# First block: both pairs of norms of the even layer and of its MLP taken in two waves of tokens

## What is computed

```python
def rms_norm(x, g): return x * lax.rsqrt(jnp.mean(x * x, -1, keepdims=True) + EPS) * g
# layer i = 0; the same for the context with its own shifts, scales and gates
h = modulate(rms_norm(x, norm_g[0, 0]), sh1, sc1)
y = even_mixer(h, hc, ...)                         # ends in a product with ev_w_out
x = x + gt1 * rms_norm(y, norm_g[0, 1])            # norm pair A: norm of y ...
h = modulate(rms_norm(x, norm_g[0, 2]), sh2, sc2)  # ... then norm of the new x
x = x + gt2 * rms_norm(squared_relu_mlp(h, mlp_w1[0], mlp_w2[0]), norm_g[0, 3])   # norm pair B
# layer i = 1
h = modulate(rms_norm(x, norm_g[1, 0]), sh1, sc1)
# odd_mixer: near = mean of the two neighbouring tokens of h, xx = near - h,
# and its keys are (h + xx * mu[2]) @ rw_wk, with five more such mixes after it
```

## Time and profile before

| | |
|---|---|
| median of 3 runs | 4765.43 us (4764.15 to 4767.18) |
| the profiled execution | 4766.37 us |
| its span, first to last instruction | 4764.6 us |
| PE busy | 4546.2 us, 95% of the span |
| DVE busy | 2705.9 us, 57% |
| ACT busy | 1044.7 us, 22% |
| POOL busy | 81.2 us, 2% |
| mean granted PE clock | 0.971 of full |
| share of PE in the chain that ended last | 87% |

### The profile page before, as it was taken

How to read it: one execution, slowest core, us unless ns; L and a number is a source line. 1 busy time by engine, 2 the same in 40 slices (tenths; PEclk the granted TensorE clock), 3 DMA queues, 4 the chain that set the end, 5 groups by cost and what they waited for, 6 DMA issues and landing times.

```text
span 4764.6 us, 70102 instructions
## 1 busy us (share of the span) xinstructions
PE 4546.2 (95%) x29830; PEld 3211.4 (67%) x29830; DVE 2705.9 (57%) x4827; ACT 1044.7 (22%) x2337; POOL 81.2 (2%) x81
## 2 busy tenths in 40 slices
PE   7999999998999999999999999989999999989998
PEld 4556555555546676756886888545887888545886
DVE  3163445535336777744565666674657666674656
ACT  1052000002016666631002100251001000151000
POOL 0000000000000000000000000110000000020000
PEclk9998999998999999998999999989999999989999
DMA  5301222210200000111222212211222212211221
GB/s 240 124 28 53 89 102 101 112 75 36 84 1 3 3 3 3 38 46 71 89 89 74 89 71 80 106 36 71 89 89 80 89 71 80 102 40 71 89 89 45
DMA packets 27045, 339.08 MB, mean 71 GB/s; under 512 B 3024, under 2 KB 3024, under 8 KB 6896
## 3 DMA queue, kind: packets, MB, share of 16 engines
q1 hardware_dynamic: 24048, 324.51, 18.1%
q0 software_dynamic: 2688, 10.09, 0.6%
HBM read 330.40 MB, written 4.19 MB: 70 GB/s over the span
## 4 chain that ended last, share of the span: by engine, by line
PE 87%; DVE 7%; ACT 3%; issue 2%; DMA 1%; SPq 0%; ACTq 0%; DVEq 0%
PE ps L1402 46%; PE ps L1086 22%; PE ps L1095 2%; PE ps L1602 1%; PE ps L1182 1%; PE ps L1533 1%; PE ps L1574 1%; PE ps L1585 1%; PE ps L1139 1%; ACT arena L1856 1%; PE ps L1340 1%; PE ps L1662 1%; PE ps L1471 1%; DVE arena L2951 1%; DMA arena<-in_panels 1%
## 5 line engine op out<-in xcount | busy, mean ns | idle before, releaser
L1402 PE MATMUL ps<-arena 128*128 128x256 f32 (+1 forms) x9096 | 2118.3, 395 | 20.8 <-DVE arena L2707 20.8
L1402 PEld LDWEIGHTS ps<-arena 128*128 128x128 f32 x9096 | 1735.4, 191 | 391.4 <-DVE arena L2707 23.6
L1086 PE MATMUL ps<-arena 128*128 128x512 f32 (+3 forms) x2896 | 1066.6, 529 | 2.2 <-ACT arena L1807 1.8
L1086 PEld LDWEIGHTS ps<-arena 128*128 128x128 f32 x2896 | 542.0, 191 | 514.7 <-issue 366.1
L2698 DVE TENSOR_TENSOR arena<-ps,arena 128x512 f32<-128x512 f32 (+1 forms) x250 | 157.6, 630 | 318.7 <-PE ps L1402 317.0
L2698 DVE TENSOR_TENSOR square<-ps,square 128x512 f32<-128x512 f32 (+1 forms) x145 | 99.1, 684 | 177.3 <-PE ps L1402 177.2
L2639 DVE TENSOR_TENSOR arena<-arena 128x1024 f32<-128x1024 f32 (+2 forms) x153 | 190.5, 1245 | 8.7 <-ACT arena L1807 5.4
L1997 ACT COPY square<-ps 128x512 f32<-128x512 f32 (+1 forms) x65 | 37.2, 573 | 658.0 <-PE ps L1402 589.1
L1997 ACT COPY arena<-ps 128x384 f32<-128x384 f32 (+1 forms) x35 | 18.5, 529 | 575.1 <-PE ps L1402 549.2
L2959 DVE COPY_PREDICATED arena<-const,ps 128x256 f32<-128x256 int32 x192 | 83.8, 445 | 74.9 <-PE ps L1602 69.4
L1856 ACT ACTIVATE arena<-arena,state_sum 128x256 f32<-128x256 f32 (+2 forms) x128 | 76.5, 598 | 213.7 <-DVE state_sum L2426 211.7
(11 more groups left out here) (348 smaller groups left out, 4924.5 us busy)
## 6 DMA issues: line engine op xcount, KB each, us to landing
arena<-in_panels SPq DMA_DIRECT2D x144, 2048.0 KB, 7.7
arena<-in_panels SPq DMA_DIRECT2D x9, 1536.0 KB, 6.4
arena<-in_bias POOLq DMA_DIRECT2D x8, 512.0 KB, 4.5
arena<-in_x_in SPq DMA_DIRECT2D x1, 3072.0 KB, 11.1
x_save<-arena POOLq DMA_DIRECT2D x1, 2048.0 KB, 7.5
arena<-x_save POOLq DMA_DIRECT2D x1, 2048.0 KB, 13.0
out_x<-arena SPq DMA_DIRECT2D x8, 256.0 KB, 2.2
arena<-in_panels SPq DMA_DIRECT2D x1, 1792.0 KB, 11.7
```

Source lines behind the costliest of these rows:

```text
L1086: ins = pe.matmul(dest, left(k), right(k), start=(k == 0), stop=(k == nk - 1))
L1402: ins = pe.matmul(bank[:, j * cut.side:(j + 1) * cut.side], left[:, k, j * P:(j + 1) * P], right[k], start=(k == 0), stop=(k == cut.rows - 1))
```

## The change

It replaces project, post and norm_mod at turn A by one step, out_turn, and the last down group, post and norm_mod(1, 0) at turn B by the same code inside mlp and odd_in. The tokens are split as WAVES: latents (512), then context (256). In PE's order, from the diff:

- Both panels of the closing product are held at once (load_pair; SLOT is changed for the panels of turn A so that they lie in slots 1 and 2 and the first up panel in slot 0; their slots are given free only when all 16 tiles are done). All eight chunks of latents come first, then the eight of context. After the first chunk of context PE makes the latents' first sum (wave_sum "post"), after the second their row, after the seventh the second sum ("norm"), after the eighth the second row. DVE and ACT do the latents' additions, squares and gates between the emptying of the context's tiles.
- Squares for the second norm are gathered too: POOL adds chunks 1 to 6 (norm_gather), so the second sum takes 16 records for the latents and 8 for the context instead of 96 together.
- The context's two sums and two rows lie inside the next product over the latents: at turn A inside the first up panel (first_up: four chunks together, sums and rows after k = 0, 2, 4, 6, then the context of the panel), at turn B inside the keys (after k = 1, after the first panel, and inside the second panel).
- POOL saves X after the latents' addition; the waits on x_chunk elsewhere are recounted.

```diff
-                SLOT.append(p % RING)
+                SLOT.append(p % RING if p < MLP_PANEL[0] - 2 else p - MLP_PANEL[0] + 3)
+        WAVES = ((0, LAT), (LAT, TOK))
-            e["project"](2, SEG2, Y, Z, "attn")
-            e["post"](Z, 0, 1)
-            e["norm_mod"](0, 2)
+            e["out_turn"]()
...
+            def turn(src):                                    # PE
+                latents, context = WAVES[0:1], WAVES[1:2]
+                w0 = panel()
+                columns(w0, range(4), src, latents)
+                w1 = panel()
+                columns(w1, range(4), src, latents)
+                columns(w0, [0], src, context)
+                wave_sum("post", 0)
+                columns(w0, [1], src, context)
+                wave_row(0)
+                columns(w0, [2, 3], src, context)
+                columns(w1, [0, 1, 2], src, context)
+                wave_sum("norm", 0)
+                columns(w1, [3], src, context)
+                wave_row(0)
...
+            def first_up(w):                                  # PE, turn A
+                banks = [tile() for _ in range(4)]
+                for k in range(KD):
+                    pe.wait_ge(sem("h_act"), more("h_act"))
+                    for m, bank in enumerate(banks):
+                        ins = pe.matmul(bank, w[:, k, m * P:(m + 1) * P], H[:, k, 0:LAT], start=(k == 0), stop=(k == KD - 1))
...
+                    if k == 0:
+                        wave_sum("post", 1)
+                    elif k == 2:
+                        wave_row(1)
+                    elif k == 4:
+                        wave_sum("norm", 1)
+                    elif k == 6:
+                        wave_row(1)
+                together(w, range(4), H, WAVES[1:2], "h_act")
...
                 for k in range(KD):                           # PE, odd_in
                     pe.wait_ge(sem("mix"), more("mix"))
...
+                    if k == 1:
+                        wave_sum("post", 1)
+                wave_row(1)
+                w1 = panel()
+                columns(w1, [0, 1], MIX, WAVES[0:1])
+                wave_sum("norm", 1)
+                columns(w1, [2], MIX, WAVES[0:1])
+                wave_row(1)
+                columns(w1, [3], MIX, WAVES[0:1])
+                together(w0, range(4), MIX, WAVES[1:2], "mix")
+                columns(w1, range(4), MIX, WAVES[1:2])
...
+            def norm_gather(v):                               # POOL
+                for c in range(1, KD - 1):
+                    pool.wait_ge(sem("squared"), base + c + 1)
...
+                    pool.tensor_tensor(rstd[:, a:b], rstd[:, a:b], square[:, c % 2, a:b], ALU.add).then_inc(
...
+            def turn(src, evacuate):                          # DVE
+                for c in range(KD):
+                    evacuate(c, *WAVES[0])
+                    wave_gather(c - 1, 0)
+                evacuate(0, *WAVES[1])
+                wave_root(0)
+                evacuate(1, *WAVES[1])
+                dve.wait_ge(sem("row"), more("row"))
+                for c in range(KD):
+                    wave_times(src, c, 0)
+                    if c > 0:
+                        wave_add(src, c - 1, 0, n["own"] - 1)
+                    if c % 2 == 1:
+                        evacuate(2 + c // 2, *WAVES[1])
+                        wave_gather(1 + c // 2, 1)
+                wave_add(src, KD - 1, 0, n["own"])
+                evacuate(6, *WAVES[1])
+                wave_gather(5, 1)
+                wave_root(0)
+                evacuate(7, *WAVES[1])
+                wave_gather(6, 1)
+                dve.wait_ge(sem("row"), more("row"))
```

More of the change, by code:

```diff
@@ L1199, in gathered_sum, with wave_sum @@
                 ins.then_inc(sem("summed"), one("summed"))
+            def wave_sum(kind, v):
+                a, b = WAVES[v]
+                squares, gathered = dict(post=("square", "gathered"), norm=("squared", "norm_gathered"))[kind]
+                stat_bank_free()
+                pe.wait_ge(sem(squares), more(squares, KD))
+                pe.wait_ge(sem(gathered), more(gathered, KD - 2))
+                for t in range(a // P, b // P):
+                    for c in (0, KD - 1):
+                        ins = pe.matmul(ps[:, 4, 0:TILES], square_dest(c)[:, t * P:(t + 1) * P], to_column(t),
+                                        start=(t == a // P and c == 0), stop=(t == b // P - 1 and c == KD - 1))
+                ins.then_inc(sem("summed"), one("summed"))
@@ new lines, in wave_row @@
+            def wave_row(v):
+                a, b = WAVES[v]
+                pe.wait_ge(sem("spread"), more("spread"))
+                for t in range(a // P, b // P):
+                    ins = pe.transpose(token_row(TOK)[:, t * P:(t + 1) * P], rstd[:, t * P:(t + 1) * P], ident)
+                ins.then_inc(sem("row"), one("row"))
+            def turn(src):
[13 more added lines that the diff above has]
+                wave_row(0)
@@ L1355, in mlp @@
                     kind, g, part = item
+                    if beside and (kind, g) == LAST_DOWN:
+                        if part == 0:
+                            pe.wait_ge(sem("half_hidden"), ends[g][0])
+                            pe.wait_ge(sem("tile_free"), ends[g][1])
+                            turn(hidden1[g % 2])
+                        continue
                     w = panel()
@@ L1370, in mlp @@
                         between = None
[L1371 to L1375, removed]
+                    if beside and item == ("up", 0, 0):
+                        first_up(w)
+                    elif not fast:
+                        columns(w, range(4), src, segs, KD, None if kind == "down" else "h_act")
                     if kind == "up":
@@ L1906, in mlp @@
                         continue
+                    if beside and (kind, g) == LAST_DOWN:
+                        if part == 0:
+                            turn(Y, 3, 1, 0)
+                        continue
                     fast = cuts(item, FF1_GROUPS, beside)
@@ new lines, in out_turn, with evacuate @@
+            def out_turn():
+                def evacuate(c, a, b):
+                    dve.tensor_copy(Z[:, c, a:b], tile()[:, 0:b - a]).then_inc(sem("tile_free"), one("tile_free"))
+                turn(Z, evacuate)
+                for c in range(KD):
+                    wave_scale(c, 0)
+                wave_root(1)
+                dve.wait_ge(sem("row"), more("row"))
+                wave_result(Z, 1)
+                wave_root(1)
+                dve.wait_ge(sem("row"), more("row"))
+                for c in range(KD):
+                    wave_scale(c, 1)
+                n["h_act"] += 2 * KD
+                n["square"] += 2 * KD
+                n["gated"] += 2 * KD
+                n["squared"] += 2 * KD
```

265 lines of the change are left out of this document (219 added, 46 removed).

## The result

The kernel after took **4726.23 us** (median of 5, 4720.35 to 4728.06) beside 4766.43 (4764.15 to 4768.05, 5 runs) of the kernel before: a ratio of 0.9913, 95% interval 0.9903 to 0.9923. It is faster by 40.2 us, where the prediction's two gains came to 50.1. The profiled execution took 4725.82 us.

A forecast was written before the change was run, and what follows sets the result against it. PE bounds the kernel, idle at turns A and B for 39.0 and 41.2 us plus clock losses. Gains of 23.9 and 26.2 us off the median 4765.4 gave 4715.3 us; forecast band 4710 to 4721, wide range 4705 to 4730.

The forecast's parts named there:

- Splitting the products costs nothing: Both turns: records of 512 and 256 columns take 0.645 us together against 0.647 for two of 384; eight chunks stay 82.6.
- Sums and rows: Each turn: two sums and two rows for latents and for context, 8.2 us of PE, all on the path.
- The latents' second sum: Both turns: POOL's clashes cost DVE 0 to 4.9 us, mostly absorbed by waits for tiles; 0.2 us of stall taken.
- The context's sum in first_up: Turn A, middle of the first up panel: 1.2 us of stall from DVE's gathers, clashes with POOL and a square.
- Handover behind the second row at A: Turn A: PE waits 1.6 us for the first chunk of H: one scale, two left-over gates and one modulation.
- The four banks: Turn A, end of first_up's latents: PE waits 4.2 us for four banks, behind ACT's modulations, relus and a DVE product.
- The clock: Each turn: 2.5 us lost to the low clock behind the long wait, nothing charged for short waits.
- Edits costed at nothing: Both turns: moved panel loads and POOL's save of the latents are covered by other work and cost nothing.
- Rival 1: POOL's additions become the last term of a sum, price 6 to 10 us: 4721 to 4726; chance 0.13.
- Rival 2: Handover waits are smaller and the clock doesn't fall: 4705 to 4710; chance 0.13.
- Rival 3: Handovers are longer through a missed wait in ACT's or DVE's order, 5 to 10 us a turn: 4726 to 4738; chance 0.10.
- Rival 4: Low clock lasts behind the turns' rows, products at 1.2 GHz, up to 124 us lost: 4839; chance 0.04.

The follow-up runs named there:

- Experiment 1: Kernel after with each of POOL's additions for the second norms cut to 64 columns, so those sums are partial: 4717.5 us, run once.
- experiment 4: Kernel after with DVE's gatherings of the context's first-norm squares moved behind the latents' last addition, ACT's squares and gates moved to match: 4720.67 us, run once.
- experiment 8: Kernel after with late gatherings, latents' relus between the context's modulations, and a key tile emptied one mix earlier, together: 4710.31 us, ratio 0.9880.
- experiment 7: The kernel after, unchanged, measured again on another chip: 4723.54 us, ratio 0.9909 to the kernel before.

## Why the prediction came out as it did

The direction was right, and so was where the gain lies; 4715.3 was 11 us too low. The time lies in the wide range, 4705 to 4730, and outside the forecast's own band of 4710 to 4721, which had been given 0.58: two terms were too small in each turn. By the steps of the forecast:

- **Splitting the products costs nothing**: right. The eight chunks of latents and the first of context take 58.65 us, 8 x 6.87 + 3.45 = 58.4.
- **Sums and rows**, 8.2 us a turn: too high. The records read 1.68 + 0.44 for the latents' first, 1.92 + 0.44, 0.79 + 0.23 and 1.03 + 0.23: 6.8 us, and 6.5 in turn B, where neither sum of the context stands behind a wait. The row of 0.77 in the earlier trace rows is four transposes with a little waiting in it; set among products they take 0.44.
- **The latents' second sum**, 0.2 us of stall: wrong, 1.84 in A and 1.83 in B. This step failed in its reasoning. The size of the clash was bounded rightly: six additions cost DVE 3.9 us, of up to 4.9 allowed (0.49 on the 1.17, 1.07 on the 1.75, and so on). Wrong was "of which the waits for tiles absorb most". The prediction's own numbers say otherwise: two chunks of 1.2 and a tile of 0.35 + 0.33 are 3.1 us of every 3.45, so the slack is 0.3 a tile. Experiment 1 has just these 0.30 us waits in its timeline, and ends at 79.7 without the clash. The clash of 3.9 less the three waits of 0.30 that it uses up is 3.0 us, and the additions end at 82.7, past the 82 us that the prediction named as the mark of its failure.
- **The context's sum in first_up**, 1.2 us: 0.67, by another last term. POOL's six additions, 0.74 + 0.13 us each, end at 459.26. DVE's, each held up by one of them (0.62 instead of 0.41), let the last square end at 459.13, so they are late almost as much.
- **Handover behind the second row at A**, 1.6 us: 2.12, with DVE's tile copy and gathering ahead of the first scale, which the forecast left out (experiment 4). **Keys' first mix at B**, 4.5: 4.61. **The four banks**, 4.2: 4.41, and with the products of DVE as the last link as said. **The banks at B**, 2.2: 2.64. The four queues written out one instruction after the other were right to 0.5 us.
- **The clock**, 2.5 us a turn, "nothing for the short ones": the larger error, 3.2 us a turn. The rows that the forecast used show a wait of 4.61 us and the two turns, and I took the short ones as free. Waits of 1.84 and 2.12 us were followed by a fall that costs as much as the wait itself. The long wait had been read low as well: 34 records in 10.60 us, against 34 x 0.216 = 7.3 at full clock, are 3.2 us lost and not 2.7.
- **Edits costed at nothing**: right. No load and no save of POOL appears in either turn as what PE waits for.

In turn A the errors are +1.6 (sum), +3.2 (clock), +0.5 (handover), +0.2 (banks), -0.5 (context's sum) and -1.4 (sums and rows), 3.6 of the 4.1 us by which the turn missed its 141.8; in B +1.6, +3.2, +0.5 and -1.7, 3.6 of 3.9. So part of the two misses was made good by sums and rows that had been priced too high, and that was luck. The rest of the 10 us between the forecast gain and the measured one is 1.9 us of start and scatter.

**Rival 1**, which had been given 0.13, came closer than the forecast. The upper end of its time, 4721 to 4726, is the one measured, its "1 to 2 us late" is what the sum shows, and POOL's sixth addition ends at 427.48, 82.1 us into the turn, "near 82" as it says. But POOL's additions are the last term only at the context's sum; at the latents' it is DVE's last addition, which ends 0.55 behind POOL's. And the clock falls, the larger part of the miss, are in none of its terms. **Rival 2** (no falls) is what experiment 8 comes near to. **Rival 3** didn't happen beyond 0.5 us. **Rival 4**, the lasting low clock, didn't happen: each fall was over after 3.4 us, and the longest that I found in the experiments' turns after 6.8, far from the 50 us that it needed.

The Trainium skill (SBUF — State Buffer, "Who interferes with whom") says that whichever of the two engines issues first keeps the shared ports for the whole instruction, and that the other is blocked. The prediction took this as a whole POOL addition lost each time, and held 1.49 us a pair against it; by that reading, as an estimate, six additions would have cost DVE 6 x 1.2 = 7.2 us, and they cost 3.9. That reading was wrong, and not the rule. The trace agrees with the rule itself: DVE's additions of 512 columns ended 0.54 or 0.55 us behind POOL's, however long they had stood (1.16 to 1.75 us), because only the rest of POOL's addition is waited for. The stretch of the earlier trace rows shows the same: POOL's third addition there ends at 3112.53 + 1.36 = 3113.89, DVE's third at 3112.86 + 1.58 = 3114.44. It bears out the restriction to SBUF inputs too: L2707, with one input in PSUM, kept its 0.68 us.

What stays open: why the same wait is followed by a fall in one execution and not in another (below), and how little the clash can be made to cost: it depends on where POOL's additions start in DVE's list (3.9 us in the kernel after, 2.2 with the same six in experiment 4). Neither handover wait was shortened by more than about 0.1 us in an experiment.

## What to carry to other kernels

When norms are set beside products, write the list of each helper engine between two of PE's wants and add it up: what counts is the slack per tile, and of a clash on top of a list that is 90% full nearly all arrives (3.0 of 3.9 us here). Ask of each instruction in front of a wanted one whether anybody needs it yet; moving four early gatherings back ended DVE's list at 80.0 us, taking the whole clash with POOL away at 79.7. And look for short waits of PE in front of dense products: those near 2 us cost about twice their length here, in all cases but one. Four of the six waits of 1.8 us or more, taken away or shortened by moving instructions alone, gave 13 us with not one operation removed.

## What the hardware showed that was not expected

- **Short waits cost a clock fall, but not by length alone.** Over the nine profiles (the kernel after, and the eight experiments), by place: a wait of 1.83 us before a sum, a fall in 10 of 10; 2.01 to 2.13 at the handover of A, 7 of 8; 4.4 at the end of first_up, 6 of 6; 2.59 at the same place, 0 of 2; 2.64 at the keys' context, 6 of 6; 4.6 at the handover of B, 8 of 8; 0.99 and less, none. The price of one is 1.7 to 2.8 us. So 2.59 us without a fall stands beside 1.83 with one, and one program (after, and experiment 7) did both at 2.12. In experiments 1, 4 and 7, where one fall of turn A stayed out, the one at the end of first_up cost more (16.25 to 16.63 us instead of 15.74), so about 0.5 to 0.9 of the 1.8 saved came back. In all three that dearer fall began while PE still waited (in experiment 7 the clock is at 0.50 from 469.5 on, and PE goes on at 471.15).
- **A clash of DVE and POOL is waiting for the rest of the other's instruction.** For additions with both inputs in SBUF, DVE's end 0.54 or 0.55 us (512 columns) or 0.28 us (256) behind the end of the POOL addition during which they were issued: 416.97 + 0.77 = 417.74 against 415.88 + 1.59 = 417.47, for one. It came to 0.65 us on DVE for each POOL addition in the kernel after and to 0.37 in experiment 4. POOL's additions took 1.59 us when a DVE addition had just started and 1.27 when one was about to end.
- **Restarting PE has a small price of its own**: a sum of 16 records takes 1.68 us behind products and 1.92 behind a wait, one of 8 takes 0.79 and 1.03.
